# Moving operand and result of the up and down projections walked as two interleaved runs

## The reference

```python
# first block: D_FF = 2816
h = rms_norm(x, norm_ffn_pre)
u = causal_dwconv(h @ w_up, conv_ffn_w)      # up: 1024 -> 2 * 2816
a, g = jnp.split(u, 2, axis=-1)
f = (gelu(g) * a) @ w_down                   # down: 2816 -> 1024
x = x + rms_norm(f, norm_ffn_post)
...
# second block: D_FF_2 = 4096
hn = rmsnorm(h, norm_mlp_g_2)
x = h + jnp.square(relu(hn @ w_up_2)) @ w_down_2   # 1024 -> 4096 -> 1024
```

## Time and profile before

| | |
|---|---|
| median of three executions | 902.0 us (901.87 to 902.0) |
| span of the profiled execution, first to last instruction | 900.7 us |
| TensorE busy (matmuls) | 888.3 us, 99% of the span |
| weight loads busy | 821.5 us |
| VectorE, ScalarE, GpSimd busy | 571.0, 496.2, 136.0 us |
| granted TensorE clock | 1.000 |

### The profile page before, as it was taken

How to read it: one execution, slowest core, us unless ns; L and a number is a source line. 1 busy time by engine, 2 the same in 40 slices (tenths; PEclk the granted TensorE clock), 3 DMA queues, 4 the chain that set the end, 5 groups by cost and what they waited for, 6 DMA issues and landing times.

```text
span 900.7 us, 15634 instructions
## 1 busy us (share of the span) xinstructions
PE 888.3 (99%) x6451; PEld 821.5 (91%) x6451; DVE 571.0 (63%) x824; ACT 496.2 (55%) x771; POOL 136.0 (15%) x151
## 2 busy tenths in 40 slices
PE   8999999999999999999999999999999999999998
PEld 8999999889999988788899988999999899998886
DVE  4556554878888746666767797765467655554542
ACT  5576864556656634566776764423454565554330
POOL 6011101611111100133443110000100011110000
PEclk9999999999999999999999999999999999999999
DMA  7843364665665566346544546542345656656560
GB/s 279 275 155 118 95 227 150 232 207 181 199 199 179 188 210 214 131 169 242 182 141 144 160 133 177 155 135 77 115 140 191 187 168 202 193 187 204 181 200 23
DMA packets 132594, 156.33 MB, mean 174 GB/s; under 512 B 9353, under 2 KB 106028, under 8 KB 132268
## 3 DMA queue, kind: packets, MB, share of 16 engines
q1 hardware_dynamic: 125844, 151.78, 51.9%
q10 hardware_dynamic: 6680, 3.56, 1.3%
HBM read 153.08 MB, written 2.24 MB: 172 GB/s over the span
## 4 chain that ended last, share of the span: by engine, by line
PE 83%; DVE 8%; DMA 3%; ACT 3%; issue 1%; POOL 1%; SPq 0%; ACTq 0%; POOLq 0%
PE ps L1979 72%; PE ps L1934 4%; PE ps L2010 3%; DVE wl L828 2%; PE ps L1931 2%; PE ps L2235 2%; DVE gv L862 1%; DVE gkq L862 1%; DMA U<-blocks 1%; DMA raw<-in_w_in 1%; DMA blocks<-last 1%; DVE mt L1267 1%; DMA Yc<-inverses 1%; ACT wh L1426 1%; DMA inverses<-Y 0%
## 5 line engine op out<-in xcount | busy, mean ns | idle before, releaser
L828 DVE TENSOR_TENSOR wl<-raw,wh 128x1024 fp32r<-128x1024 f32 (+1 forms) x275 | 326.4, 1205 | 190.0 <-ACT wh L1426 189.9
L1979 PE MATMUL ps<-xh,wh 128*128 128x256 f32 x1280 | 357.3, 282 | 0.7 <-ACT xh L1474 0.7
L1979 PE MATMUL ps<-xh,wl 128*128 128x256 f32 x1280 | 350.6, 277 | 0.0
L1426 ACT ACTIVATE wh<-raw 128x1024 fp32r<-128x1024 f32 (+1 forms) x292 | 286.6, 1024 | 115.4 <-PE ps L1979 93.0
L1979 PE MATMUL ps<-xl,wh 128*128 128x256 f32 x1280 | 348.3, 277 | 0.0
L1979 PEld LDWEIGHTS ps<-xh,wh 128*128 128x128 f32 x1280 | 238.9, 188 | 4.5 <-issue 1.4
L1979 PEld LDWEIGHTS ps<-xh,wl 128*128 128x128 f32 x1280 | 238.8, 188 | 0.0
L1979 PEld LDWEIGHTS ps<-xl,wh 128*128 128x128 f32 x1280 | 238.0, 188 | 0.3
L669 POOL TENSOR_TENSOR wl<-raw,wh 128x1024 fp32r<-128x1024 f32 (+1 forms) x17 | 44.2, 2600 | 81.6 <-ACT wh L1426 81.3
L1979 PE MATMUL ps<-wh,f2L 128*128 128x512 f32 x128 | 49.8, 389 | 0.0
L1979 PE MATMUL ps<-wl,f2H 128*128 128x512 f32 x128 | 49.8, 389 | 0.0
(11 more groups left out here) (334 smaller groups left out, 1363.8 us busy)
## 6 DMA issues: line engine op xcount, KB each, us to landing
raw<-in_w_in SPq DMA_DIRECT2D x55, 1024.0 KB, 5.1
raw<-in_w_up SPq DMA_DIRECT2D x38, 1024.0 KB, 5.2
raw<-in_w_down SPq DMA_DIRECT2D x26, 1024.0 KB, 5.0
raw<-in_w_out SPq DMA_DIRECT2D x8, 1024.0 KB, 5.1
raw<-in_w_proj_fox SPq DMA_DIRECT2D x4, 1024.0 KB, 5.1
raw<-in_w_proj_gdn SPq DMA_DIRECT2D x4, 1024.0 KB, 5.1
raw<-in_w_conv_branch SPq DMA_DIRECT2D x4, 512.0 KB, 3.4
raw<-in_w_att_branch SPq DMA_DIRECT2D x4, 512.0 KB, 3.3
```

The lines of the kernel that those rows point to most:

```text
L828: e.tensor_tensor(L, R, H.bitcast(F32), ALU.subtract).then_inc(lo.sem)
L1426: e.activation(tile_of(WH, u)[:, k:kc, :], tile_of(RAW, u)[:, k:kc, :], ACT.Copy).then_inc(hi.sem)
L1979: k = e.matmul(o, l, r, start=opens, stop=done and n == ends[c], skip_group_check=True)
```

## The change

In the four stages the last access dimension of the moving operand and of the result is split in two halves, and the walk takes a run of e elements from the first half, the next e from the same place in the second half, and so on. Source and destination are walked in the same order, so every result element lands where it did. e is 16 in the first up projection, 4 in the first down projection, 2 in the second up and 32 in the second down projection. The halves are 128 elements (512 bytes) apart in mode B and 256 elements (1024 bytes) apart in mode A. Nothing else changes: same instructions, same number, same waits. The three units that `part` does keep their plain walk.

```diff
+            def two_runs(ap, e):
+                return ap.rearrange("p (h b e) -> p b h e", h=2, e=e)
+
+            def run_of(u):
+                if U_UP <= u < U_DN:
+                    return 16
+                if U_DN <= u < AHEAD2[0]:
+                    return 4
+                if U_UP2 <= u < U_DN2:
+                    return 2
+                return 32 if u >= U_DN2 else None
...
                     l, r = (W[:, cs], X) if mode == "B" else (X[:, cs], W)
+                    if run_of(u):
+                        o, r = two_runs(o, run_of(u)), two_runs(r, run_of(u))
                     k = e.matmul(o, l, r, start=opens, stop=done and n == ends[c], skip_group_check=True)
```

## The result

The changed kernel takes 959.6 us (956.15 to 960.05, four executions) against 902.0 before. The ratio is 1.0624, 95% interval 1.0612 to 1.0637: 6.2% slower, and past the upper end of my range.

What follows compares the result with a forecast made beforehand. The prediction took TensorE's unbroken matmul stream to bound the kernel in the four changed stages. With zero for each switch the sum was 0 us, so 902.0 us, own range 900.5 to 903.5; the whole range was 882 to 946.

Steps and rivals of the forecast that it cites:

- What bounds the kernel: In the four changed stages TensorE is busy without a gap, so each nanosecond of matmul distance is kernel time; together 337.7 us.
- I take zero for each switch: All four stages: switching between halves costs nothing, 0 us, giving 902.0 us; chance of nothing measurable 0.38.
- short runs pay: Second up projection first, then first down: runs of 2, perhaps 4, cost extra; +43.5 or +101.7 us; chance 0.25.
- The 64-byte reading: Each run pays anew one cycle for stepping to the next 64 bytes: first down +7.7, second up +35.8, sum +43.5 us.
- the 128-byte reading: Each run pays two cycles, as for each 128 bytes: first up +7.0, first down +17.9, second up +76.8, sum +101.7 us.
- The lost cycle of 17: Four stages: plain matmuls take 17 cycles for 16 columns, 272 for 256 and 544 for 512, so one cycle is lost.
- the pace falls to 18 for 16: All four stages: the new walk holds the first unit's pace, 120.0 and 240.0 ns; +19.2 us, 921.2; chance 0.07.
- any stepped result is written at half rate: All four stages: writing the result in two pieces runs at half rate; about +323 us, 1225; chance 0.04.
- the lost cycle goes: Four stages: matmuls reach 16 cycles for 16 columns; -20.3 us, or -7.6 if weight loads hold the up stages; chance 0.26.
- the floor for 256 columns: Up stages: weight loads may set a floor of 111.3 ns, so only the down stages gain fully, 7.6 us, 894.4.
- The rule on lines: SBUF lines of 16 bytes need two hits, PSUM lines have 8 bytes; runs of 2 satisfy this, so the sum is zero.
- The two paces: Same shapes ran at 118.5 and 113.4 ns, or 233.0 and 228.9, so addresses and their timing set the pace.

Runs made afterwards that it cites:

- plain_up2: The changed kernel without its runs of 2, so the second up projection is walked in plain order: 918.35 us, ratio to before 1.0171.
- write_only: Against the changed kernel, only the result is written in two interleaved runs and the moving operand is read plainly: 902.80 us, ratio to before 0.9999.
- The sweeps: Kernels whose run length changes from unit to unit, with read and write stepped or the read alone; distances were measured, 111.6 ns for 256 columns with runs of 1.
- turns_four: Kernel before, with moving tiles stored in halves and read in turn in the two feed-forward parts alone: 892.13 us, ratio 0.9885.
- phase_64: Moving tiles XH and XL placed 64 bytes higher, only the read stepped, run length varied; plain distance 120.0 ns where it had been 113.3.
- read_only: Against the changed kernel, only the moving operand is read in two interleaved runs and the result is written plainly: 957.54 us, ratio to before 1.0612.
- turns_A: Kernel before, with WH and WL stored in halves and read in turn wherever a weight is the moving operand: 902.57 us, ratio 1.0000.
- turns_AB: As turns_A, with XH and XL also stored in halves and read in turn in the two up projections: 896.26 us, ratio 0.9923.

## Why the prediction was wrong, point by point

**What bounds the kernel** was right. TensorE's stream is the whole of the four stages, and each ns of distance went into the time: +6.7, +4.5, +36.9, +3.9 us by the windows, 52 of the 53.7 us of the spans; plain_up2 gave back 41.2 us for one stage, and write_only, whose distances are those of before, took the time of before.

**The step that failed** is "I take zero for each switch". It rested on the measured jumps of the earlier trace rows, which cost nothing. Those matmuls make one jump in 256 columns and stream at half the rate, and I had written down myself that this is slack the others lack and that no row shows a short run; I then weighed neither. The sweeps show that the first point matters by itself: at the full rate of fp32r, 512 columns in runs of 64 or 128 still take 226.7 ns, so jumps that come seldom are free there too. Whether the slack of the fp32 matmuls would have hidden short runs as well was not tested. In its place the runs showed a cost in the read of the moving operand for every run length from 2 to 32: 51 to 57 ns in 256 columns for pairs, 23.3 in 512 for runs of 4, 6.7 in 256 for runs of 16 and 10 in 512 for runs of 32, together the 52 us.

**The rival "short runs pay"** named the side and the main place rightly (the second up projection first), and had the sign. Its form was wrong in both readings. The 64-byte reading gave 113, 267, 160 and 227 ns for the four stages, the 128-byte reading 120, 320, 213 and 227; measured were 120.0, 250, 164.7 and 236.7. Both let runs of 32 be free, and they are not. Both make short runs the cause, and runs of 1 are the fastest walk of all. The lost cycle of 17 is not a fixed price of the next 64 bytes either: the in-turn walk comes to as many new ones and doesn't lose it.

**The rival "the pace falls to 18 for 16"** named 120.0 and 240.0 ns for all four stages. The first up stage had exactly that, and so did 512 columns with runs of 16 in the sweeps, but it is no general pace: the stages with runs of 4, 2 and 32 had 250, 164.7 and 236.7. Part of its ground was misread. I had taken 5.69 / 48 = 118.5 ns for the pace of the first up unit. From start to start only the first two distances of that unit are long, 195 and 116 ns, and the last one, up to the `settle` matmul, 205; the 45 between have a mean of 113.4, the pace of the later units. The earlier trace rows does show 233.0 ns, a real second pace. **The rival "any stepped result is written at half rate"** fell with write_only.

**The rival "the lost cycle goes"** was, for this change, wrong in sign: no stage gained. But part of that gain can be had by another walk. The cycle does go when two halves are read in turn, 215.8 ns for 512 columns, and the floor for 256 columns that I had read off the fp32 matmuls, 111.3 ns, is where the in-turn walk ends, 111.6. That the loads set this floor was not tested by itself. In turns_four the four stages gained 1.8 ns for 256 columns and 10.9 for 512, of the 6.7 and 13.3 that a walk without any loss would have given. The Trainium skill (TensorE: Matmul & The Clock Gate, section Back-to-back issue gap) gives N / 2.4 + 2.5 ns, 215.8 ns for 512 columns; the prediction called it a figure for a stream, while that section calls it the gap of an isolated matmul. The plain walk doesn't reach it, and the in-turn walk meets it in a stream.

**The rule on lines** of the Trainium skill (Advanced Engine Details and Errata, section Memory Cachelines) asks for two hits in a line of 16 bytes of SBUF, and for consecutive pairs in PSUM. The walk of pairs satisfies both by the order of its elements and still lost 51 ns of 113. The traces come nearer to two hits if they are counted among every second element of the walk, though not in every row. Its sentence that any non-contiguous pattern in PSUM slows matmuls finds no support for runs of 2 and longer: write_only had a ratio of 0.9999. Runs of 1 were not written.

**The two paces.** I had seen that the same shape has more than one pace and held it for a sign that the meeting of the two reads decides. phase_64 shows that this is so for the plain walk, by 6.7 ns. It has little to do with the change. It may account for the spread of the changed kernel: 720 matmuls at 170.0 in place of 164.5 ns are 3.9 us, the difference between its spans of 954.4 and 958.3. That is argued, since only the one execution of it was profiled; the profiled execution of read_only, with 168.2 ns in this stage, fits it.

**What stays open.** The cause below the distances. Theory A, counting by every second element, is a reading and was not shown: two readers that take turns, each with the last line it read, account for in turn, every second element and the wide walks, but not for 114.6 ns with 16 places and runs of 4 beside 135.1 with four places, nor for the slow fall from 23 to 10 ns for 512 columns between runs of 4 and 32. Why the plain walk goes at 113.3 ns in one place and at 117.9 in another, with the same tiles, is open too.

## What to carry to other kernels

Where TensorE's stream is the bound, measure the distance from start to start and hold it against one column for each cycle: here the plain fp32r walk gave away one cycle in 17, and storing the moving tile in two halves and reading one element from each in turn gave it back, 10.4 us of 902. A row that shows an operation for free shows it only as often as it was done there, and at the rate at which it ran: one jump in 256 columns said nothing of 128. Work that is moved to other engines has to be covered in every stage where it is put: with halved tiles in the attention part too, TensorE's waits ate what its matmuls had gained, and a wait of 3.6 us was followed by a stretch at half the clock. And a stream that is tried in one kernel with a different walk for each unit gives a whole table of prices in one execution.

## What the runs showed of the hardware that I had not expected

- The order of the moving read alone moves an fp32r matmul of 256 columns between 111.6 and 233.3 ns; the order of the PSUM writes, in runs of 2 and 16, moves it by nothing.
- Reading 0, 128, 1, 129 is faster than reading 0, 1, 2, 3 (111.6 against 113.3 to 117.9 ns, 215.8 against 226.7 for 512 columns), and reading 0, 1, 128, 129 is slower (164.5 to 170).
- The in-turn walk kept its 111.7 ns when the tile was moved by 64 bytes, which cost the plain walk 6.7 ns.
- Reading RAW at every second element made the conversions of the last stage slower by half on ScalarE (1052 to 1593 ns for one of 128x1024) and by a quarter on VectorE (1222 to 1522 ns).
- Right behind a stop of 3.6 us TensorE's granted clock was 0.50 in turns_A, and 512 columns took 426 ns in place of 215.8. The mean clock of an execution shows it: four of six executions of turns_AB had less, and took 2.5 us or more longer than the other two.
